# Four sums of squares in column quarters, and no products of zeros behind the first transposes

## The reference

```
def _rmsnorm(x, w):
    xf = x.astype(jnp.float32)
    y = xf * lax.rsqrt(jnp.mean(xf * xf, axis=-1, keepdims=True) + RMS_EPS)
    return (y * w.astype(jnp.float32)).astype(x.dtype)

h = h + _mixer(_rmsnorm(h, norm_mix_w[l]), ...)                                    # norm 0
h = h + _swiglu(_rmsnorm(h, norm_ffn_w[l]), w_ffn_gate[l], w_ffn_up[l], w_ffn_down[l])  # norm 1
h = _rmsnorm(h, norm_final_w)                                   # with the next one: norm 2
# second block, layers 0 and 1: mixer behind norms 2 and 4, hidden layer behind norms 3 and 5
```

## Time and profile before

| what | value |
|---|---|
| median of 3 runs | 1094.96 us (1094.09 to 1096.31) |
| the profiled execution | 1096.72 us, span 1094.9 us |
| TensorE products busy | 1075.9 us, 98% of the span |
| VectorE busy | 727.8 us, 66% |
| ScalarE busy | 526.2 us, 48% |
| loads | 177.40 MB, 162 GB/s on average |
| mean granted clock of TensorE | 0.992 |

### The profile page before, as it was taken

The page is one execution under the profiler, slowest core; times in us unless marked ns, Lnnn a source line. Parts: engine busy times, 40 slices in busy tenths (PEclk is TensorE's granted clock), DMA queues, the critical chain, the costliest instruction groups (busy, mean ns, idle before and its releaser), DMA issues.

```text
span 1094.9 us, 21043 instructions
## 1 busy us (share of the span) xinstructions
PE 1075.9 (98%) x8656; PEld 1040.0 (95%) x8656; DVE 727.8 (66%) x782; ACT 526.2 (48%) x551; POOL 2.2 (0%) x5
## 2 busy tenths in 40 slices
PE   8999999999999999999999999999999999999998
PEld 7998897899999999989989999999999999999998
DVE  5855757768666666677767656554579987555553
ACT  5521636544644444455785443342566574434431
POOL 0000000000000000000000000000000000000000
PEclk8999999999999999999999999999899999999999
DMA  9684242345556656746316655645254445556431
GB/s 309 198 226 132 78 135 78 124 147 180 161 154 200 188 172 178 236 152 202 116 57 214 196 188 169 210 158 162 70 158 150 149 163 183 199 186 198 157 111 39
DMA packets 162590, 177.40 MB, mean 162 GB/s; under 512 B 4800, under 2 KB 148288, under 8 KB 162536
## 3 DMA queue, kind: packets, MB, share of 16 engines
q1 hardware_dynamic: 160704, 174.33, 50.3%
q10 hardware_dynamic: 1832, 2.30, 1.1%
HBM read 175.04 MB, written 1.57 MB: 161 GB/s over the span
## 4 chain that ended last, share of the span: by engine, by line
PE 82%; DVE 12%; ACT 4%; issue 1%; DMA 1%; SPq 0%; DVEq 0%; ACTq 0%
PE proj L449 52%; PE aux L869 22%; DVE wlo L1599 4%; DVE f L1602 2%; DVE f L1599 2%; PE aux L507 2%; ACT whi L1137 1%; PE aux L624 1%; DMA f<-in_x_dram 1%; PE aux L739 1%; PE aux L724 0%; DVE r_all L2246 0%; DVE f L1605 0%; PE aux L609 0%; DVE r_all L1602 0%
## 5 line engine op out<-in xcount | busy, mean ns | idle before, releaser
L449 PE MATMUL proj<-u,whi 128*128 128x256 f32 (+1 forms) x2912 | 533.1, 285 | 2.3 <-DVE f L1599 1.5
L1599 DVE TENSOR_TENSOR wlo<-raw,whi 128x2048 fp32r<-128x2048 f32 (+2 forms) x179 | 374.6, 2093 | 138.6 <-ACT whi L1137 127.5
L449 PEld LDWEIGHTS proj<-u,whi 128*128 128x128 f32 x2912 | 452.0, 190 | 7.6 <-issue 5.8
L449 PE MATMUL proj<-u,wlo 128*128 128x256 f32 (+1 forms) x1456 | 411.9, 283 | 0.0
L1137 ACT ACTIVATE whi<-raw 128x2048 fp32r<-128x2048 f32 (+2 forms) x173 | 309.6, 1790 | 106.0 <-PE aux L869 40.3
L449 PEld LDWEIGHTS proj<-u,wlo 128*128 128x128 f32 x1456 | 276.9, 190 | 0.0
L869 PE MATMUL aux<-v,whi 128*128 128x256 f32 x1376 | 249.7, 283 | 1.3 <-DVE v L1599 1.3
L869 PEld LDWEIGHTS aux<-v,whi 128*128 128x128 f32 x1376 | 214.2, 192 | 1.5 <-issue 1.5
L869 PE MATMUL aux<-v,wlo 128*128 128x256 f32 x688 | 194.6, 283 | 0.0
L869 PEld LDWEIGHTS aux<-v,wlo 128*128 128x128 f32 x688 | 131.9, 192 | 0.0
L449 PE MATMUL proj<-v,whi 128*128 128x256 f32 (+1 forms) x564 | 103.8, 286 | 0.9 <-DVE f L1599 0.8
(11 more groups left out here) (283 smaller groups left out, 717.1 us busy)
## 6 DMA issues: line engine op xcount, KB each, us to landing
raw<-in_mlp_w_dram SPq DMA_DIRECT2D x64, 1024.0 KB, 5.4
raw<-in_w_in_dram SPq DMA_DIRECT2D x21, 1024.0 KB, 6.3
raw<-in_od_w_in_dram SPq DMA_DIRECT2D x12, 1024.0 KB, 5.4
raw<-in_w_ffn_gate_dram SPq DMA_DIRECT2D x22, 512.0 KB, 4.0
raw<-in_w_ffn_up_dram SPq DMA_DIRECT2D x22, 512.0 KB, 5.2
raw<-in_w_ffn_down_dram SPq DMA_DIRECT2D x21, 512.0 KB, 5.4
raw<-in_ev_w_in_dram SPq DMA_DIRECT2D x10, 1024.0 KB, 6.0
raw<-in_w_ret_out_dram SPq DMA_DIRECT2D x4, 1024.0 KB, 5.4
```

What stands on the lines that cost most here:

```text
L449: ins = mm(o, w_of(a, k), x_of(b, k), start=first and k == 0 and j == 0, stop=last and k == kt - 1 and j == 2, skip_group_check=skip)
L1599: return ve.tensor_tensor(o, a, b, op)
```

## The change

Norms 0, 1, 3 and 5 get another form of the sum. A product of the squares with a 128 x 32 piece of the ones fills one quarter of the output partitions. Feature blocks 0 to 3 go to the four quarters, and blocks 4 to 7 are added on top. After that every quarter holds a sum over two of the eight feature blocks, repeated 32 times. ScalarE copies this to `r_all`, and one product of the copy with the whole matrix of ones adds up all 128 partitions; the result is 32 times too large, which the scale of the root takes back. In norms 1, 3 and 5 the four products of each half come before feature blocks 4 and 6, the product of the copy behind feature block 7. In norm 0 all eight come behind `rq0`, the product of the copy before feature block 4 of `rq1`.

The five products of zeros behind the transposes go. VectorE takes `rq0` and `rq1` out of PSUM before it splits the chunk that it split ahead of them so far. The semaphore of the zeros is merged with that of the small constants, and the two of the last transposes with each other.

```
@@ tensor
+            def square_half(c, norm_no):
+                pe.wait_ge(sems["sq_ready"], 4 * norm_no + 2 * c + 2)
+                for k in range(4 * c, 4 * c + 4):
+                    part = slice(32 * (k % 4), 32 * (k % 4) + 32)
+                    ins = mm(aux[part, 0, 0:S], C("ones")[:, 0:32], sq_of(S)[:, k, :], start=c == 0, stop=c == 1, skip_group_check=True)
+                if c == 1:
+                    ins.then_inc(sems["sum_parts"], 1)
+
+            def whole_sum(norm_no):
+                pe.wait_ge(sems["parts_kept"], norm_no // 2 + 2)
+                mm(aux[:, 0, 0:S], C("ones"), r_all[:, 0, 0:S], start=True, stop=True).then_inc(sems["sumsq"], 1)
+
+            def by_half(norm_no):
+                def gate(k):
+                    if k in (4, 6):
+                        square_half(k // 2 - 2, norm_no)
+                    if k % 2 == 0:
+                        pe.wait_ge(sems["u_ready"], 4 * norm_no + k // 2 + 1)
+                return gate
...
-            pe.wait_ge(sems["warm_ready"], 1)
+            pe.wait_ge(sems["small_ready"], 2)
...
-            for j in range(WARM // 2):
-                mm(proj[:, 0, 0:P], warm, warm, start=True, stop=True)
...
-            for c in range(4):
-                square_pair(c, 0, L)
-            project("rq1", t0=META, t=S)
+            pe.wait_ge(sems["sq_ready"], 4)
+            for k in range(KT):
+                part = slice(32 * (k % 4), 32 * (k % 4) + 32)
+                ins = mm(aux[part, 0, 0:L], C("ones")[:, 0:32], sq[:, k, :], start=k < 4, stop=k >= 4, skip_group_check=True)
+            ins.then_inc(sems["sum_parts"], 1)
+
+            def token_sums(k):
+                if k == 4:
+                    pe.wait_ge(sems["parts_kept"], 1)
+                    mm(aux[:, 0, 0:L], C("ones"), r_all[:, 0, :], start=True, stop=True).then_inc(sems["sumsq"], 1)
+
+            project("rq1", t0=META, t=S, gate=token_sums)
...
+                        if between and j == 0:
+                            between()
...
-                up(g, 0, gate=by_pair(norm_no))
+                up(g, 0, gate=by_half(norm_no), between=lambda: whole_sum(norm_no))
@@ scalar
             pump(index["rq0"] - AHEAD + 2)
+            eng.wait_ge(sems["sum_parts"], 1)
+            A.post(act(r_all[:, 0, :], aux[:, 0, 0:L], ACT.Copy), "parts_kept")
             eng.wait_ge(sems["sumsq"], 1)
-            root(aux[:, 0, 0:L], r_all[:, 0, :], 1.0 / D, eps, "root_ready")
+            root(aux[:, 0, 0:L], r_all[:, 0, :], 1.0 / 32 / D, eps, "root_ready")
...
+                if isinstance(source, str):
+                    eng.wait_ge(sems["sum_parts"], norm_no // 2 + 2)
+                    A.post(act(r_all[:, 0, 0:S], aux[:, 0, 0:S], ACT.Copy), "parts_kept")
                 eng.wait_ge(sems["sumsq"], norm_no + 1)
-                root(aux[:, 0, 0:S], r_all[:, 0, 0:S], 1.0 / D, eps_ap, "root_ready")
+                scale = 1.0 / 32 / D if isinstance(source, str) else 1.0 / D
+                root(aux[:, 0, 0:S], r_all[:, 0, 0:S], scale, eps_ap, "root_ready")
@@ vector
             for c in range(2):
-                b = arrive(f"rq{c}")
+                b = arrive(f"rq{c}", urgent=True)
                 freed(tt(preq[:, 2 * c:2 * c + 2, :], proj[:, b:b + 2, 0:S], bc(rq, 2), ALU.mult))
+                pump(index[f"rq{c}"])
...
```

More of the change, by code:

```diff
@@ L844, in hidden_layer, with up @@
                 turn = bank_turn[tag]
-                def up(n, k, i=None, gate=None):
+                def up(n, k, i=None, gate=None, between=None):
                     pe.wait_ge(sems["lo_ready"], at(lambda m: m + 1, n, i))
@@ L1116, in _ @@
                     if k % 4 == 3:
-                        ins.then_inc(sems["left_turned" if b == 0 else "right_turned"], 1)
+                        ins.then_inc(sems["out_turned"], 1)
         @block.scalar
@@ L1576, in _ @@
             for j in range(2):
-                eng.wait_ge(sems["left_turned"], j + 1)
+                eng.wait_ge(sems["out_turned"], 2 * j + 1)
                 A.post(act(f("f4", 1024 * j, 512), proj[:, j, :], ACT.Copy), "left_ready")
@@ L1642, in _ @@
             B.post(ve.memset(one, 1.0), "small_ready")
-            B.post(ve.memset(warm, 0.0), "warm_ready")
+            B.post(ve.memset(warm, 0.0), "small_ready")
             def keep(k):
@@ L2327, in _ @@
             for j in range(2):
-                eng.wait_ge(sems["right_turned"], j + 1)
+                eng.wait_ge(sems["out_turned"], 2 * j + 2)
                 B.post(ve.tensor_copy(f("f4", 1024 * j + 512, 512), proj[:, 2 + j, :]), "right_ready")
```

## The result

The changed kernel takes 1087.2 us (median of four runs, 1086.1 to 1089.8) against 1094.5 of the kernel before on the same chip, a ratio of 0.9938 with a 95% interval of 0.9921 to 0.9956. Predicted were 1087.8, between 1085.0 and 1092.0.

The account below looks back on a forecast made before the run. TensorE was taken to bound the kernel, its products being 82% of the span. Terms 1.2 + 1.96 + 0.33 + 2 x 1.51 + 0.65 = 7.16, say 7.1, took 1094.96 to 1087.8 us, range 1085.0 to 1092.0.

Parts of the forecast that it names:

- The zeros: Behind the front's transposes: without the zeros `rq0` begins 2.15 us earlier, gaining 1.2 if the clock rises at the same moment.
- Norm 0: Between `rq0` and `rq1`: eight quarter products at 1.25 us and the copy's product at 0.46 replace 3.67, gaining 1.96.
- The rival without overlap: At the four norms: quarter products do not run side by side, each costing 0.433 us as now; 1097.5 us, chance 0.06.
- The two chunks taken out first: In the front: VectorE takes results out before its split, so `rk0` does not wait; 0.33 us on TensorE.
- Norms 1 and 3: Block 0 to the second output block falls from 6.30 to 4.79 us, gaining 1.51 each, with no wait on the copy.
- Norm 5: Block 0 to the second output block takes 5.65 against 6.30 us, gaining 0.65; the wait on `u` replaces the squares.
- What is late next: Behind norm 3, hidden values keep 0.5 us to spare; behind the front, loads, splits and copies come earlier too, so gains stand.
- The front was not given back: Rival: behind `rv1`, the wait on `gamma_rows` ends at a fixed time and takes the front's 3.5 us; 1091.3, chance 0.11.
- the clock did not fall: Rival: quarters and waits bring half clock at each of three hidden layers, 3.4 us each; 1098.1 us, chance 0.05.
- signs to look for: In the trace: `rq0` within 0.1 of the last transpose, norm 0's records within 1.1 to 1.2 us, `rk0` without idle entry.

Follow-up runs that it names:

- zeros_back: The changed kernel with the five products of zeros put back behind the transposes: 1088.54 us.
- result_late: The changed kernel with VectorE splitting a chunk ahead of the first two results again, as before the change: 1089.44 us.
- no_cover: The changed kernel with the product of the copy moved ahead of feature blocks 6 and 7 at norms 1, 3 and 5: 1091.96 us.
- split_behind: The changed kernel with VectorE's last split ahead of norm 5 moved behind the last two blocks of `u`: 1089.22 us.

## Why the prediction was right

**The zeros.** Predicted 1.2, measured 1.15 in the two traces whose clock rose at nearly the same time (19.16 and 18.96). The reckoning (what is done at half clock while the zeros would run) is borne out by zeros_back, for its own times. That the clock rose at the same moment was an assumption, and that it held in these two executions is luck (the tokens landed 0.20 later and the clock rose 0.20 earlier, which cancel). What the prediction did not say is that the term can vanish: where the clock is high, it is 0.08.

**Norm 0.** Predicted 1.96, measured 1.97. The price of eight quarters, 1.25, came from a row of the same shape elsewhere in the kernel and not from a rule. The rival without overlap had a sentence of the Trainium skill behind it ("TensorE: Matmul & The Clock Gate", Part 3, The mechanism), by which a weight load overlaps running products only where the row groups differ. These traces do not agree: all products here use all the rows, and sixteen records take 1.12, their sixteen weight loads 0.61 within it.

**The two chunks taken out first.** Predicted 0.33, measured 0.32. But that is no price of the edit by itself: worked out against the old order it is 0.33, within the new one 1.71 (result_late). The prediction put down the 0.33 as the edit's worth and did not see this. Its sum came out because in the final order nothing waits, and not because three parts have three fixed prices.

**Norms 1 and 3.** Predicted 1.51 each, measured 1.50: 4.79 for the first output block with its sums, and 7.63 - 2.84 = 4.79 measured. That the copy has just enough cover was right: without it 0.65 is lost (no_cover), against the 0.67 reckoned.

**Norm 5.** Predicted 0.65, measured 0.65, and for the reason given: with the split out of the way the norm gains the full 1.50 (split_behind).

**What is late next.** Nothing was, as predicted. The front was not given back at `gamma_rows` (3.40 of 3.44), and the clock did not fall at norms 1, 3 and 5 of the changed kernel. Behind norm 3 the hidden values end at 599.05 and TensorE comes at 599.52, so 0.47 is left, where 0.5 was reckoned. The one miss of the signs to look for: `rq0` began 0.2, not 0.1, behind the start of the last transpose.

**The total.** 7.1 predicted in the profiled execution, 6.9 measured. The median came out 0.6 below the forecast; with runs from 1085.84 to 1091.46 this difference says nothing about the parts. The total alone would also have come out with other parts; the table of stages is what tests the account.

## What to carry to other kernels

Where a chain is one engine, price a new form from a row of the same shape elsewhere in the trace, and then walk along every consumer in the final order: an edit that looks worth 0.3 alone can be what lets another one's 2 us through. Put short extra work where the engine would wait anyway, not where it is tidiest. And before runs are compared, look at the granted clock stage by stage: two places in this kernel made up nearly the whole spread between runs.

## What the runs showed of the hardware that was not expected

- Behind norm 4, where TensorE runs products of 8 columns, the granted clock fell to 0.50 for 3.4 to 17 us in all eleven profiled runs that have them, and in none of the three with 128 columns. In the changed kernel TensorE counted as busy without a gap just before the fall, from 778.00 to 780.10. Both kinds start 0.112 apart, so the wider ones cost nothing.
- Four products to different quarters of the output columns run side by side even if they are not neighbours in the program. In the cases run here the fullest quarter sets the time (8 records in 0.64 over four quarters, 1.06 over two).
- With twelve products of zeros in TensorE's idle 2.8 us the clock of the front stayed at 1.00 in all three profiled runs that have them; in the eleven without them it fell to 0.50. The five behind the transposes of the kernel before come too late for that: they begin at 13.74, and the clock had fallen at 8.91.
